# Expert tail and the next mixer's projections in one block, the value projection first, norm weights applied at the transposed copy

## The chip, the cores and the metric

One core of one Trainium2 chip runs the program. The metric is device time in microseconds of one execution, as the median of several runs; lower is better.

## What is computed

Three layers run one after another on 512 tokens of 1024 channels, all in float32: a hybrid mixer (state space and attention), a differential-attention mixer, and an RWKV-7 time mix. Each layer is a mixer, a norm, a mixture of experts with two experts per token, and a second norm.

```python
x = layer_norm(ALPHA * x + mixer(x), ln1_g, ln1_b)
f = hier_moe(x, ...)                 # out = sum over 2 experts of weight * (act @ w_down)
x = layer_norm(ALPHA * x + f, ln2_g, ln2_b)
# layer_norm: (x - mean) * rsqrt(var + 1e-5) * g + b
# differential attention: q, k, v = split(x @ w_qkv, 3)
# time mix: xx = shift(x) - x;  xm[n] = x + xx * mu[n]
#   r, k, v = xm[0..2] @ w_rkv[0..2];  w, a, g from xm[3], xm[4], xm[5] through narrow matrices w1, a1, g1
```

## The kernel before

Tokens lie in four tiles of 128 (`NT` = 4); `x_tok` holds them with tokens on the partitions and `xT` (in `xt_mem`) holds the transposed copy, eight blocks of 128 channels (`NK` = 8) by 512 tokens. Weights come in chunks of 2 MB (1024 rows by 512 columns) through `ring`, which has six slots; SP issues their loads in the order of a list, `stream`, and waits before each for the job that used the slot last (`used`). `first` is the list's first chunk of a mixer.

The program is a row of blocks. All engines meet at the end of a block before any starts the next. Around the change they are these.

- `project_and_experts` (L877) ends with a block of expert loops. In it the two rows of each token are written to the buffer `xybuf` in device memory; ACT's last stores must have landed before the block ends.
- The **tail** is the second block of the same function (L1300 to L1358). POOL gathers the expert rows of each tile by two indirect DMAs, eight in all (L1320), and behind the first pair it loads the norm weights as rows broadcast to all partitions, two loads of 512 KB (L282, L283). ACT scales `x_tok` by alpha (L1330). For each tile DVE adds the two weighted rows (L1347, L1348) and measures mean and variance (L222, L224); ACT takes the square root (L247); DVE normalizes (L229, L230) and multiplies by g (L231); POOL adds b (L252), for the last tile DVE (L234). DVE does a tile's measuring before it normalizes the tile before. PE turns each finished tile (L267, eight transposes of 128x128), ACT copies the result from PSUM in two activations (L273). SP loads three more chunks of the next mixer when all gathers have landed (L163); the first three came during the expert loops.
- `qkv_stage` (L1369) is the next block for the second layer: 24 jobs of PE, each eight k-steps into one PSUM bank (L1403), 16 for q and k, then 8 for v; ACT evacuates (L1414) and begins with an exponential for lambda (L1409).
- `rkv_stage` (L1464) is the next block for the third layer. ACT issues eleven parameter loads (L1546), PE turns the small parameters (L1513), DVE computes the token shift `xx` (L1498, L1499) and then six mixes of eight operations each (L1506), in the order w, a, g, r, k, v. PE runs four narrow jobs w, a, g, g2 (L1527), 16 jobs for r and k (L1539) and 8 for v (L1536), ACT evacuates (L1573).
- In the last layer nothing follows the tail, and SP stores each finished tile (L1313).

The first norm of each layer, in the expert stage, already works in another way: DVE makes scale and shift of a tile (L1169, L1170), ACT applies them in one activation (L1117), PE turns the tile (L1008), and DVE multiplies by g and adds b later (L1175, L1176). PE's projection jobs there are L1035.

## Time and profile before

| | us |
|---|---|
| median of 3 runs | 2915.38 (2912.75 to 2915.76) |
| the profiled execution, its own time | 2915.37 |
| its span in the trace | 2913.6 |

The span is the profiled stretch on the core; a row with a start time counts from its beginning. PE is TensorE's matmuls, PEld its weight loads, DVE is VectorE, ACT ScalarE, POOL GpSimd and SP SyncE. An arrow names what ended an engine's idle time.
### The profile page before, as it was taken

How to read it: one execution, taken by the hardware profiler on the slowest of the kernel's cores; microseconds unless marked ns; L12 is line 12 of the kernel's file. 1: busy time of each engine (PE TensorE's matmuls, PEld its weight loads, DVE VectorE, ACT ScalarE, POOL GpSimd, SP SyncE). 2: the span in 40 equal slices, each digit the busy share in tenths (PEclk: the TensorE clock that was granted, in tenths of full speed). 3: DMA queues.
4: the chain of work that ended last, by engine and by line, in shares of the span. 5: the costliest groups of instructions: out<-in, count | busy, mean ns of one | idle time of the engine just before them, and what ended most of it. 6: DMA issues, size and time to landing. Idle time of an engine off the chain costs nothing. (4 is left out here: it accounts for less than half of the span.)

```text
span 2913.6 us, 88815 instructions
## 1 busy us (share of the span) xinstructions
PE 2390.6 (82%) x39032; PEld 1652.3 (57%) x39033; DVE 1080.5 (37%) x2763; ACT 480.8 (17%) x1070; POOL 167.0 (6%) x254
## 2 busy tenths in 40 slices
PE   8987897999679978799866719988887889788972
PEld 3436656777534554577645513438787357566751
DVE  0205534333330284433311254016665743222325
ACT  1023411101110241110000010013333110000001
POOL 0000010000110000000000030001111200000002
PEclk9988899999889999999988959989999699899986
DMA  6211217987332101979999950000000349999994
GB/s 232 87 58 49 85 49 295 385 350 315 135 118 87 58 1 33 384 315 393 428 429 428 428 199 29 29 0 3 3 3 14 145 156 402 429 428 428 413 429 168
DMA packets 84523, 613.58 MB, mean 211 GB/s; under 512 B 20178, under 2 KB 41938, under 8 KB 50596
## 3 DMA queue, kind: packets, MB, share of 16 engines
q1 hardware_dynamic: 41440, 567.30, 47.0%
q10 hardware_dynamic: 36356, 22.86, 2.6%
q0 software_dynamic: 6592, 21.45, 2.3%
q8 instruction: 106, 1.74, 0.2%
q14 instruction: 29, 0.24, 0.0%
HBM read 579.04 MB, written 32.51 MB: 210 GB/s over the span
## 5 line engine op out<-in xcount | busy, mean ns | idle before, releaser
L1084 PE MATMUL ps<-ring,arena 128*32 128x128 f32 x13440 | 414.1, 282 | 110.7 <-DMA ring<-in_experts 80.9
L1084 PEld LDWEIGHTS ps<-ring,arena 128*32 128x32 f32 x13440 | 384.9, 114 | 152.0 <-DMA ring<-in_experts 78.9
L1061 PE MATMUL ps<-x_tok,arena 128*32 128x256 f32 x4832 | 305.2, 392 | 20.9 <-DVE arena L1198 16.7
L1284 DVE TENSOR_TENSOR arena<-arena,ps 128x64 f32<-128x64 f32 x296 | 65.6, 222 | 631.5 <-ACT arena L1143 631.5
L1143 ACT ACTIVATE arena<-ps 128x64 f32<-128x64 f32 x296 | 66.1, 223 | 1159.7 <-PE ps L1084 1159.7
L1061 PEld LDWEIGHTS ps<-x_tok,arena 128*32 128x32 f32 x4832 | 165.9, 114 | 103.8 <-issue 34.7
L1084 PE MATMUL ps<-arena 128*32 128x128 f32 x5504 | 178.8, 291 | 47.0 <-DMA arena<-in_experts 39.0
L1094 PE MATMUL ps<-ring,arena 128*32 128x256 f32 x3360 | 203.3, 380 | 8.4 <-DMA ring<-in_experts 8.1
L1084 PEld LDWEIGHTS ps<-arena 128*32 128x32 f32 x5504 | 163.4, 117 | 67.4 <-DMA arena<-in_experts 46.3
L1035 PE MATMUL ps<-ring,arena 128*128 128x512 f32 x384 | 168.4, 594 | 3.1 <-PEq L192 3.1
L1094 PEld LDWEIGHTS ps<-ring,arena 128*32 128x32 f32 x3360 | 112.9, 110 | 81.0 <-DMA ring<-in_experts 16.0
L1271 DVE STREAM_TRANSPOSE arena<-ps 128x256 f32<-128x256 f32 x151 | 67.9, 450 | 162.2 <-PE ps L1061 162.2
L1035 PEld LDWEIGHTS ps<-ring,arena 128*128 128x128 f32 x384 | 71.5, 190 | 87.2 <-issue 86.9
L1403 PE MATMUL ps<-xt_mem,ring 128*128 128x512 f32 x256 | 111.9, 600 | 0.9 <-PEq L1302 0.9
L1539 PE MATMUL ps<-arena,ring 128*128 128x512 f32 x256 | 110.1, 592 | 0.0
L453 PE MATMUL ps<-xt_mem,ring 128*128 128x512 f32 x256 | 110.0, 592 | 0.0
L846 DVE TENSOR_REDUCE small<-ps 128x1 f32<-128x128 f32 (+3 forms) x96 | 46.7, 486 | 167.5 <-PE ps L757 165.6
L1320 POOL DMA_INDIRECT arena<-xybuf,arena x24 | 24.1, 1004 | 1363.8 <-POOLq L951 861.0
L1295 DVE COPY arena<-ps 128x256 f32<-128x256 f32 x148 | 62.8, 425 | 88.0 <-PE ps L1094 88.0
L1094 PE MATMUL ps<-xt_mem,arena 128*32 128x256 f32 x1376 | 83.4, 380 | 6.5 <-DMA xt_mem<-in_experts 4.8
L1403 PEld LDWEIGHTS ps<-xt_mem,ring 128*128 128x128 f32 x256 | 49.3, 193 | 63.2 <-issue 63.2
L1539 PEld LDWEIGHTS ps<-arena,ring 128*128 128x128 f32 x256 | 48.6, 190 | 61.6 <-issue 61.6
(405 smaller groups left out, 3098.4 us busy)
## 6 DMA issues: line engine op xcount, KB each, us to landing
ring<-in_experts SPq DMA_DIRECT2D x165, 2048.0 KB, 22.1
arena<-in_experts SPq DMA_DIRECT2D x50, 2048.0 KB, 25.9
xt_mem<-in_experts SPq DMA_DIRECT2D x25, 2048.0 KB, 30.2
ring<-in_mixer_chunks SPq DMA_DIRECT2D x24, 2048.0 KB, 12.5
xybuf<-arena ACTq DMA_DIRECT2D x640, 32.0 KB, 6.7
xybuf<-arena SPq DMA_DIRECT2D x1, 9216.0 KB, 25.7
rows<-in_ln_g POOLq DMA_DIRECT2D x6, 512.0 KB, 5.2
rows<-in_ln_b POOLq DMA_DIRECT2D x6, 512.0 KB, 6.5
```

Of the source, the lines that this page charges most:

```text
L453: ins = pe.matmul(bank, w[:, k, j * P:(j + 1) * P], xT[:, k, :], start=(k == 0), stop=(k == NK - 1))
L846: link(dve.tensor_reduce(m[:, c:c + 1], score(n, c), AX, ALU.max))
L1035: ins = pe.matmul(ps[:, 2 * j + c, :], mT[:, k, j * P:(j + 1) * P], w[:, k, :], start=(k == 0), stop=(k == NK - 1))
L1061: ins = pe.matmul(ps[to, 5, 0:W], one_hot[:, j, :], x_tok[:, j, q * W:(q + 1) * W], start=(j == 0), stop=(j == NT - 1))
L1084: ins = pe.matmul(ps[at, 2 + half, 0:P], xg[:, k, :], w_gu[half][:, k, q, :], start=(k == 0), stop=(k == NK - 1))
L1094: ins = pe.matmul(ps[at, 4, 0:W], hT[:, f, :], w_d[:, f, q * W:(q + 1) * W], start=(f == 0), stop=(f == NT - 1))
L1143: act.activation(silu_g[:, half, :], ps[:, 2 + half, 0:HALF], ACT.Silu).then_inc(s_silu[half], 1)
L1271: dve.transpose(xg.rearrange("p k s -> p (k s)"), ps[:, 5, 0:W]).then_inc(s_xg, 1)
L1284: dve.tensor_tensor(hidden[:, half, :], silu_g[:, half, :], ps[:, 2 + half, HALF:P], ALU.mult)\
L1295: dve.tensor_copy(y_sb[:, b, :], ps[:, 4, 0:W]).then_inc(s_y, 1)
L1403: ins = pe.matmul(ps[:, n % 8, :], lhs, rhs, start=(k == 0), stop=(k == NK - 1))
L1539: ins = pe.matmul(bank, w[:, k, j * P:(j + 1) * P], xm[:, k, :], start=(k == 0), stop=(k == NK - 1))
```

## The change

For layers two and three the tail and the projection stage become one block (`norm_qkv_stage`, `norm_rkv_stage`); the last layer gets `last_norm_stage`. The chunks of the second and third mixer are listed with the value weights first. For each tile PE turns x as normalized but without g and b; ACT copies the turned tile in eight activations that apply g and b as columns (`take_rows`), and `x_tok` gets g and b from DVE afterwards (`gain_rows`). PE puts the turning of tile n+1 behind value job n. The norm rows and columns are loaded by POOL in the expert block. Gathered rows lie in ring slots. The third layer's parameters are loaded by SP into a ring slot at the block's start, and the value mix is made tile by tile. The exponential for lambda is moved to the end of its stage. "..." marks what is left out.

```diff
-            stream += [a["mixer_chunks"][8 * n + c] for c in range(8)]
+            stream += [a["mixer_chunks"][8 * n + c] for c in ((0, 1, 2, 3, 4, 5, 6, 7) if n == 0 else (4, 5, 0, 1, 2, 3, 6, 7))]
...
+        def gather_rows(pool, y1, y2, slots_i):
+            for j in range(NT):
+                for n, y in enumerate((y1, y2)):
+                    pool.indirect_dma_start(out=y[:, j, :], out_offset=None, in_=xybuf,
+                                            in_offset=bass.IndirectOffsetOnAxis(ap=slots_i[:, n, j:j + 1], axis=0))\
+                        .then_inc(rows_in[j].sem, 16)
+        def alpha_rows(act, alpha):
+            for j in range(NT):
+                act.activation(x_tok[:, j, :], x_tok[:, j, :], ACT.Copy, scale=alpha).then_inc(act_a.sem, 1)
+        def update_rows(dve, link, j, n0, y1, y2, w1, w2):
+            xj, mv = x_tok[:, j, :], mean_var[:, j, :]
+            dve.wait_ge(act_a.sem, n0["alpha"] + j + 1)
+            dve.wait_ge(rows_in[j].sem, n0["rows"][j] + 32)
+            link(dve.scalar_tensor_tensor(xj, y1[:, j, :], w1[:, j:j + 1], xj, ALU.mult, ALU.add))
+            link(dve.scalar_tensor_tensor(xj, y2[:, j, :], w2[:, j:j + 1], xj, ALU.mult, ALU.add))
             for c in range(2):
                 ins = dve.bn_stats(sums[:, j % 2, 6 * c:6 * c + 6], x_tok[:, j, c * CH:(c + 1) * CH])
             link(ins)
+            dve.bn_aggr(mv[:, 0:2], sums[:, j % 2, :]).then_inc(stat.sem, 1)
             dve.wait_ge(sq.sem, n0["sq"] + j + 1)
             link(dve.reciprocal(mv[:, 3:4], mv[:, 2:3]))
+            dve.tensor_scalar(mv[:, 1:2], mv[:, 0:1], mv[:, 3:4], -1.0, ALU.mult, ALU.mult).then_inc(scaled.sem, 1)
-            link(dve.tensor_scalar(xj, xj, mv[:, 0:1], mv[:, 3:4], ALU.subtract, ALU.mult))
-            ins = dve.tensor_tensor(xj, xj, g_row, ALU.mult)
-            if j == NT - 1:
-                link(ins)
-                ins = dve.tensor_tensor(xj, xj, b_row, ALU.add)
-            ins.then_inc(scaled.sem, 1)
...
+        def norm_rows(act, j, n0):
+            mv = mean_var[:, j, :]
             act.wait_ge(stat.sem, n0["stat"] + j + 1)
+            act.activation(mv[:, 2:3], mv[:, 1:2], ACT.Sqrt, bias=eps_ln).then_inc(sq.sem, 1)
+            act.wait_ge(scaled.sem, n0["scales"] + j + 1)
+            act.activation(x_tok[:, j, :], x_tok[:, j, :], ACT.Identity, bias=mv[:, 1:2], scale=mv[:, 3:4]).then_inc(ln_done.sem, 1)
+        def turn_rows(pe, j, n0):
+            pe.wait_ge(ln_done.sem, n0["normed"] + j + 1)
             for c in range(2):
                 for k in range(4):
                     at = (4 * c + k) * P
                     ins = pe.transpose(ps[:, 2 * j + c, k * P:(k + 1) * P], x_tok[:, j, at:at + P], ident)
                 ins.then_inc(tr.sem, 1)
+        def take_rows(act, j, n0):
             for c in range(2):
+                act.wait_ge(tr.sem, n0["turned"] + 2 * j + c + 1)
+                for k in range(4 * c, 4 * c + 4):
+                    ins = act.activation(xT[:, k, j * P:(j + 1) * P], ps[:, 2 * j + c, (k % 4) * P:(k % 4 + 1) * P], ACT.Identity,
+                                         scale=g_col[:, k:k + 1], bias=b_col[:, k:k + 1])
+                ins.then_inc(act_b.sem, 1)
+        def gain_rows(dve, link, j):
+            xj = x_tok[:, j, :]
+            link(dve.tensor_tensor(xj, xj, g_row, ALU.mult))
+            return dve.tensor_tensor(xj, xj, b_row, ALU.add)
...
+                    pool.wait_ge(*at_step("placed", LAST_TILE_SCALED))
+                    load_norm_rows(pool, g_src_2, b_src_2)
+                    if not last:
+                        load_norm_cols(pool, g_src_2, b_src_2)
...
+        def after_experts(n):
+            first = mixer_at[n]
+            return first, view(slot((first + 4) % SLOTS), 0, NT, D), view(slot((first + 5) % SLOTS), 0, NT, D)
+        def last_norm_stage(alpha, w1, w2, slots_i):
+            y1, y2 = view(arena, NK * T, NT, D), view(arena, 2 * NK * T, NT, D)
...
+                    def finish(j):
+                        dve.wait_ge(ln_done.sem, n0["normed"] + j + 1)
+                        gain_rows(dve, link, j).then_inc(dve_b.sem, 1)
+                    dve.wait_ge(loaded.sem, l0)
+                    for j in range(NT):
+                        update_rows(dve, link, j, n0, y1, y2, w1, w2)
+                        if j > 0:
+                            finish(j - 1)
+                    finish(NT - 1)
...
+        def norm_qkv_stage(alpha, w1, w2, slots_i):
+            first, y1, y2 = after_experts(1)
+            jobs = [(c, j) for j in range(NT) for c in range(2)] + [(c, j) for c in range(2, 6) for j in range(4)]
...
+                    load_chunk(sp, first + 3)
+                    sp.wait_ge(stat.sem, n0["stat"] + NT)
+                    for n in range(first + 4, first + SLOTS):
+                        load_chunk(sp, n)
...
+                    turn_rows(pe, 0, n0)
+                    for n, (c, j) in enumerate(jobs):
+                        if c < 2:
+                            pe.wait_ge(act_b.sem, n0["taken"] + 2 * j + 2)
+                        else:
...
+                        if n < NT - 1:
+                            turn_rows(pe, n + 1, n0)
...
+                    alpha_rows(act, alpha)
+                    act.wait_ge(loaded.sem, l0)
+                    for j in range(NT):
+                        norm_rows(act, j, n0)
+                        take_rows(act, j, n0)
+                    for n, (c, j) in enumerate(jobs):
+                        act.wait_ge(mm.sem, m0 + n + 1)
+                        dst = v2[:, j, c * CH:(c + 1) * CH] if c < 2 else (q2, k2)[(c - 2) // 2][:, 4 * (c % 2) + j, :]
+                        act.activation(dst, ps[:, n % 8, :], ACT.Copy).then_inc(ev.sem, 1)
                     act.wait_ge(dve_a.sem, x0 + 1)
+                    act.activation(sums_of, sums_of, ACT.Exp).then_inc(act_a.sem, 1)
...
+            buf = {"v": k3, "w": rT, "a": k3, "g": rT, "r": k3, "k": xx}
+            lora = slot((first + 3) % SLOTS)
+            jobs = [("v", c, j) for j in range(NT) for c in range(2)] + ["w", "a", "g", "g2"]
+            jobs += [(n, c, j) for n in "rk" for c in range(2) for j in range(4)]
...
+                    sp.wait_ge(consts.sem, c0 + 1)
+                    load(param_rows[0:6 * NK, :], a["rw_mu_2"][0].rearrange("n (k p) -> (n k) p", p=P))
...
+                    load(lora_w, a["rw_w1_2"][0].rearrange("(k p) n -> p k n", p=P))
+                    load(lora_a, a["rw_a1_2"][0].rearrange("(k p) n -> p k n", p=P))
+                    load(lora_g, a["rw_g1_2"][0].rearrange("(k p) n -> p k n", p=P))
+                    sp.wait_ge(stat.sem, n0["stat"] + NT)
+                    for n in range(first + 4, first + SLOTS):
+                        load_chunk(sp, n)
+                    sp.wait_ge(dve_b.sem, d0 + 1)
+                    load(w2a2[0:64, :], a["rw_w2_2"][0])
+                    load(w2a2[64:128, :], a["rw_a2_2"][0])
+                    sp.wait_ge(mm.sem, m0 + done["g2"])
+                    load_chunk(sp, first + 3)
...
+                    def mix_tile(j):
+                        of = slice(j * P, (j + 1) * P)
+                        if j == 0:
+                            dve.wait_ge(consts.sem, c0 + 3)
+                        dve.wait_ge(act_b.sem, n0["taken"] + 2 * j + 2)
+                        if j == 0:
+                            dve.tensor_tensor(xx[:, :, 1:P], xT[:, :, 0:P - 1], xT[:, :, 1:P], ALU.subtract)
+                            link(dve.tensor_scalar(xx[:, :, 0:1], xT[:, :, 0:1], -1.0, None, ALU.mult))
+                        else:
+                            link(dve.tensor_tensor(xx[:, :, of], xT[:, :, j * P - 1:(j + 1) * P - 1], xT[:, :, of], ALU.subtract))
+                        mix(0, of)
+                    for j in range(NT):
+                        update_rows(dve, link, j, n0, y1, y2, w1, w2)
+                        if j > 0:
+                            mix_tile(j - 1)
+                    mix_tile(NT - 1)
+                    mix(1, slice(0, T))
+                    dve.wait_ge(loaded.sem, l0)
+                    for j in range(NT):
+                        ins = gain_rows(dve, link, j)
+                    ins.then_inc(dve_b.sem, 1)
+                    for n, free_after in ((2, "v"), (3, "w"), (4, "a")):
+                        dve.wait_ge(mm.sem, m0 + done[free_after])
+                        mix(n, slice(0, T))
+                    mix(5, slice(0, T))
...
+                    pe.wait_ge(mixer_params.sem, p0 + 16 * 9)
                     pe.transpose(ps[:, 7, 0:P], param_rows, ident).then_inc(tr.sem, 1)
...
+                        if n < NT - 1:
+                            if n == NT - 2:
+                                pe.wait_ge(consts.sem, c0 + 3)
+                            turn_rows(pe, n + 1, n0)
...
+                    alpha_rows(act, alpha)
                     act.wait_ge(tr.sem, t0 + 1)
                     act.activation(mu, ps[:, 7, 0:6 * NK].rearrange("p (n k) -> p n k", n=6), ACT.Copy)
                     act.activation(par, ps[:, 7, 6 * NK:(6 + N_PAR) * NK].rearrange("p (n k) -> p n k", n=N_PAR), ACT.Copy)\
                        .then_inc(consts.sem, 1)
+                    act.wait_ge(loaded.sem, l0)
+                    for j in range(NT):
+                        norm_rows(act, j, n0)
+                        take_rows(act, j, n0)
```

## Rows read from the trace of the kernel before
**Rows 1.** The page: busy time, share of the span and instructions of each engine
```profile
PE 2390.6 (82%) x39032; PEld 1652.3 (57%) x39033; DVE 1080.5 (37%) x2763; ACT 480.8 (17%) x1070; POOL 167.0 (6%) x254
```
**Rows 2.** Timeline 774 to 800 us: start, length, engine, line, operation, [idle before <- releaser]
```profile
781.63 1.04 POOL L1320 DMA_INDIRECT arena<-xybuf,arena  x1 [345.62 <-POOLq L951]
...
788.29 1.28 DVE L1347 SCALAR_TENSOR_TENSOR x_tok<-arena,x_tok 128x1024 f32<-128x1024 f32 x1 [11.07 <-DMA arena<-xybuf,arena]
...
792.68 1.29 DVE L222 BATCH_NORM_STATS2 small<-x_tok 128x6 f32<-128x512 f32 x2 [1.79 <-DMA rows<-in_ln_b]
```
**Rows 3.** Timeline 800 to 835 us, the rest of the first tail
```profile
802.87 3.24 DVE L1348 SCALAR_TENSOR_TENSOR x_tok<-arena,x_tok 128x1024 f32<-128x1024 f32 x1
...
805.09 1.97 PE L267 MATMUL ps<-cst,x_tok 128*128 128x128 f32 x8 [28.35 <-POOL x_tok L252]
...
826.39 1.28 ACT L1409 ACT_TABLE_LOAD   x1 [0.26 <-PEq L1302]
...
826.42 8.93 PE L1403 MATMUL ps<-xt_mem,ring 128*128 128x512 f32 x16 [0.93 <-PEq L1302]
```
**Rows 4.** Timeline 1690 to 1800 us, second tail and the projections after it
```profile
1692.26 1.28 DVE L1347 SCALAR_TENSOR_TENSOR x_tok<-arena,x_tok 128x1024 f32<-128x1024 f32 x1 [11.30 <-DMA arena<-xybuf,arena]
...
1730.18 4.42 DVE L1498 TENSOR_TENSOR arena<-xt_mem 128x4088 f32<-128x4088 f32 x1 [2.95 <-PEq L1302]
...
1734.68 0.34 ACTq L1546 DMA_DIRECT2D rows<-in_rw_mu  x1
...
1746.24 0.48 PE L1513 MATMUL ps<-cst,rows 128*128 128x128 f32 x1 [16.98 <-DMA rows<-in_rw_a]
...
1752.60 15.22 PE L1527 MATMUL ps<-arena 128*64 128x512 f32 x32 [5.89 <-DVE arena L1506]
...
1762.65 10.69 DVE L1506 SCALAR_TENSOR_TENSOR arena<-arena,xt_mem 128x512 f32<-128x512 f32 x16 [4.80 <-PE ps L1527]
```
**Rows 5.** Timeline, the last evacuation of either projection stage
```profile
993.33 0.60 ACT L1414 ACTIVATE arena<-ps 128x512 f32<-128x512 f32 x1 [6.27 <-PE ps L1403]
...
1947.25 0.60 ACT L1573 ACTIVATE arena<-ps 128x512 f32<-128x512 f32 x1 [6.27 <-PE ps L1536]
```
**Rows 6.** Timeline 1125 to 1130 us, the first tile's norm in the expert stage
```profile
1125.73 0.16 DVE L1169 RECIPROCAL small<-small 128x1 f32<-128x1 f32 x1 [0.36 <-ACT small L1111]
1125.93 0.21 DVE L1170 TENSOR_SCALAR small<-small 128x1 f32<-128x1 f32 x1
...
1126.88 1.04 PE L1008 MATMUL ps<-cst,x_tok 128*128 128x128 f32 x8
...
1128.48 1.24 ACT L1117 ACTIVATE x_tok<-x_tok,small 128x1024 f32<-128x1024 f32 x1
```
**Rows 7.** Timeline 2855 to 2914 us, the last tail, DVE alone
```profile
2874.92 1.28 DVE L1347 SCALAR_TENSOR_TENSOR x_tok<-arena,x_tok 128x1024 f32<-128x1024 f32 x1 [11.91 <-DMA arena<-xybuf,arena]
...
2882.40 1.28 DVE L1347 SCALAR_TENSOR_TENSOR x_tok<-arena,x_tok 128x1024 f32<-128x1024 f32 x1 [1.40 <-DMA arena<-xybuf,arena]
...
2886.36 0.21 DVE L224 BATCH_NORM_AGGREGATE small<-small 128x2 f32<-128x12 f32 x1
...
2909.32 1.23 DVE L234 TENSOR_TENSOR x_tok<-x_tok,rows 128x1024 f32<-128x1024 f32 x1
```
**Rows 8.** Groups by shape, ACT and DVE, 128 columns: count, busy us, mean ns, idle before
```profile
L818 ACT ACTIVATE xt_mem<-ps,small 128x128 f32<-128x128 f32 x24 | 8.8, 367 | 6.9 <-DVE small L847 5.9 <-PE ps L776 0.7
...
L828 ACT ACTIVATE xt_mem<-ps 128x128 f32<-128x128 f32 x16 | 4.3, 267 | 0.0
...
L858 DVE SCALAR_TENSOR_TENSOR xt_mem<-xt_mem,small 128x128 f32<-128x128 f32 x8 | 2.8, 352 | 0.3
```
**Rows 9.** Windows: length, PE, PEld, DVE, ACT, POOL busy, TensorE clock, DMA share, GB/s
```profile
792.00:794.00 2.00, 0.00 (x0) 0.00 (x0) 1.29 (x2) 0.00 (x0) 0.94 (x1) 0.50 1.02 408
1190.00:1194.00 4.00, 3.35 (x96) 2.54 (x92) 1.28 (x5) 0.22 (x1) 0.00 (x0) 0.76 0.66 243
2398.00:2402.00 4.00, 4.00 (x120) 3.19 (x116) 1.64 (x5) 0.10 (x1) 0.00 (x0) 1.00 0.04 10
```

More of the change, by code:

```diff
@@ L216, in build, with tail_bases @@
         sums = view(lnx, 16, 2, 12)
-        def measure(dve, link, j):
+        def tail_bases():
+            return {"alpha": act_a.take(NT), "stat": stat.take(NT), "sq": sq.take(NT), "scales": scaled.take(NT), "normed": ln_done.take(NT),
+                    "turned": tr.take(2 * NT), "taken": act_b.take(2 * NT), "rows": [r.take(32) for r in rows_in]}
+        def gather_rows(pool, y1, y2, slots_i):
[13 more added lines that the diff above has]
+            link(dve.scalar_tensor_tensor(xj, y2[:, j, :], w2[:, j:j + 1], xj, ALU.mult, ALU.add))
             for c in range(2):
@@ L283, in load_norm_rows, with load_norm_cols @@
             pool.dma_start(b_row, b_src.partition_broadcast(P)).then_inc(loaded.sem, 16)
+        def load_norm_cols(pool, g_src, b_src):
+            with nc.allow_non_contiguous_dma("one value per partition"):
+                pool.dma_start(g_col, g_src.rearrange("(k p) -> p k", p=P)).then_inc(loaded.sem, 16)
+                pool.dma_start(b_col, b_src.rearrange("(k p) -> p k", p=P)).then_inc(loaded.sem, 16)
+        g_col, b_col = small[:, 8:16], small[:, 16:24]
         R_PAD = 96
@@ L1297, in project_and_experts @@
                 x.take(16 * (E // 3))
-            r0, l1, x0, n0 = loaded.take(32), [r.take(32) for r in rows_in], act_a.take(NT), norm_bases(not last)
-            o0 = stored.take(16 * NT) if last else 0
+            loaded.take(32 if last else 64)
+            return w1, w2, slots_i
+        def after_experts(n):
[3 more added lines that the diff above has]
+            y1, y2 = view(arena, NK * T, NT, D), view(arena, 2 * NK * T, NT, D)
+            n0, l0, d0, o0 = tail_bases(), loaded.total, dve_b.take(NT), stored.take(16 * NT)
             with nc.Block() as block:
@@ L1367, in build @@
         subln = rows[:, 256:256 + P]
[L1369 to L1371 removed]
+        def norm_qkv_stage(alpha, w1, w2, slots_i):
+            first, y1, y2 = after_experts(1)
+            jobs = [(c, j) for j in range(NT) for c in range(2)] + [(c, j) for c in range(2, 6) for j in range(4)]
+            n0, l0, lam0, d0 = tail_bases(), loaded.total, loaded.take(32), dve_b.take(1)
+            m0, e0 = mm.take(24), ev.take(24)
             for c in range(6):
[L1373 removed]
+                used[first + c] = (mm.sem, m0 + max(n for n, job in enumerate(jobs) if job[0] == c) + 1)
             prods = view(rows, 512, 2, HD)
[L1375 removed]
+            sums_of = cols[:, 16:18]
             x0, a0 = dve_a.take(1), act_a.take(1)
```

220 lines of the change are left out of this document (69 added, 151 removed).

## The prediction

> **What bounds the kernel now.** The page comes first: PE is busy 82% of the span [rows 1], so time is won only where PE stands still, and the change touches the three tails, where it does. In the timeline of the first tail POOL issues the first gather at 781.63, DVE begins the first tile at 788.29, and then waits 1.79 us more for the b row [rows 2]. PE's first transpose comes at 805.09 after 28.35 us of idleness, and its first projection at 826.42 [rows 3]. Between lies a chain: four tiles measured, normalized, shifted by POOL and turned, and nothing of the projection until the last has landed. One link is slow for a reason outside itself: L1348 takes 3.24 us while POOL adds b, against 1.28 for the same kind of operation in L1347 [rows 2, 3]. The second tail is the same with more behind it: DVE starts at 1692.26, the shift is computed from 1730.18, the first parameter load is issued at 1734.68, PE turns the parameters at 1746.24, having waited 16.98 us for a load, and its first job starts at 1752.60 [rows 4]. Both projection stages are then bound by PE: ACT evacuates a bank every 6.27 + 0.60 = 6.87 us, to the last at 993.33 and 1947.25 [rows 5]. So in either stage the question is when the first job starts, what is put between jobs, and what stands behind the last. The last tail has no projection; DVE's own chain ends it.
>
> **Layer two, start of the first job.** A tile's update by DVE runs from 2882.40 to the end of the aggregate at 2886.57 [rows 7], 4.17 us; behind it come ACT's root (0.36 idle), the reciprocal 0.16 and the scale 0.21 [rows 6], with a 0.04 handoff 0.77: **4.94 us an update**. Then ACT normalizes, 1.24 [rows 6], 0.1 for the handoff. PE turns the tile in 1.97 us at the 1.2 GHz that it has after idling (the same eight took 1.04 at 2.4 GHz) [rows 3, 6]. Then eight small copies stand where two wide ones stood. The trace has no copy with both scale and bias columns; the nearest are 0.267 us with none and 0.367 with a column [rows 8]. I take 0.35 apart; four of them overlap the second half of the turning but end about 0.5 after it, four more need 1.4, so about 2.0 behind PE.
> The start of the update moves too. SP now issues a 2 MB chunk at the block's start, where before it waited for the gathers. At the 408 GB/s that the DMA engines reach when full [rows 9] it takes 5.1 us. If the gather's packets come first it costs nothing, if the chunk goes first 5.1; a gain is excluded, since nothing that stood before the first pair is removed. I take 2.5, the middle, since both are in flight at once. So 788.3 + 2.5 + 4.94 + 1.34 + 2.0 + 2.0 = **801.1** for the first job against 826.4: 25.3 us won. It starts cold as before (8.93 for the first sixteen instructions [rows 3]), so that loss is in both.
> Between jobs PE turns tiles 1 to 3: 3 x 1.04 = 3.1 us back. They do not wait: tile 1 is normalized at about 804, during the first job; tile 2's root waits on ACT for the copies of tile 1, some 2 us after that turn, and is done inside the second job of 6.87. The v weights are there, for the first three chunks came in the expert loops. Behind the last job the exponential for lambda comes with its table load, 1.28 [rows 3], and four short steps of the size of those in [rows 6], 0.8 together: 2.1 back. DVE's g and b (8 operations of 1.23 [rows 7]) and the lambda loads queued behind them on POOL lie beside 165 us of matmuls. Layer two: 25.3 - 3.1 - 2.1 = **20.1 us**.
>
> **Layer three.** The parameters are loaded while rows are gathered, by SP, 1.2 MB up to the narrow matrices. Before, the whole set needed 11.6 us from first issue to PE's transpose [rows 4]. Issued from about 1685.6 (as far ahead of DVE's first update as in the first tail, 6.7 us [rows 2]), they land at 1697 at that pace, and ACT needs them before its first root, at 1698.4 (their copy is queued ahead of it). If all 4 MB of gathers went first, 10.3 us at 408 GB/s, they would come at 1707 and hold all back by 8.8. Bounds 0 and 8.8; I take 2, since most of the set is small and both queues move together. First tile copied: 1692.3 + 2 + 4.94 + 1.34 + 2.0 + 2.0 = 1704.6. DVE's second update is measured by then, but its root stands behind those copies: 1705.4. Only then comes the value mix of tile 0: a quarter of the shift (4.42 / 4 = 1.1 [rows 4]), 0.3 for the first column, and eight operations of at most 0.352 [rows 8], 0.3 apart with overlap: 3.8. First job at **1709.2** against 1752.6: 43.4 won.
> From there DVE needs about 8 to 9 us a tile (4.17 to measure, a wait for ACT, 3.5 to 3.8 to mix), and PE has two jobs and a transpose a tile, 14.8, so mixes stay ahead. Mix w (half of 10.69 us for 16 [rows 4]) and g and b are done before the eight v jobs end. Mix a can start only when v is done, as it reuses that buffer, and takes 5.3 beside job w of 6.87; g and r likewise. Their cover is thin, 1.5 us. Chunk first+3 is loaded only after g2, with four r jobs, 27.5 us, to hide it. The three turns cost 3.1 again: 43.4 - 3.1 = **40.3 us**.
>
> **Last tail.** The norm rows no longer stand between gathers, 1 MB at 408 GB/s, 2.5 us: the second tile's update starts at 2879.9 instead of 2882.40, just when the first is done (2874.92 + 4.94). Then three updates, 14.8, and four times g and b at 2.46, 9.8 (ACT normalizes beside them), end at 2904.6. Before it was 2909.32 + 1.23 = 2910.55 [rows 7]: **5.9 us**. POOL's adding was free there but slowed L1348; doing it on DVE costs less than it returns.
>
> **Expert blocks.** Each takes up 1 MB of norm rows, and small columns, when the routing is done. In the third layer the DMA engines carry 10 GB/s in 2398 to 2402, so there is room. In the second a third of the capacity was free in 1190 to 1194 (share 0.66), about 1.4 us of the 2.5 [rows 9]. Bounds 0 and 3 x 2.5 = 7.5; I take 0.5, as loads run well ahead of use at that point.
>
> **The sum.** 20.1 + 40.3 + 5.9 - 0.5 = 65.8. The profiled execution took 2915.37, as much as the median, and 1.8 us of it lie outside its span: 2915.4 - 65.8 = **2849.6**.
>
> **A rule beside the rows.** In the second tail the narrow matrices w1 and a1 arrive in rows of 64 floats, 256 bytes, 0.5 MB together. The Trainium skill, DMA: Bandwidth & Descriptors, Specifications, gives 512 bytes as the least for full rate. By that rule these two cost about twice their bytes, some 1.3 us more of DMA time, and the sum would be 2850.9; no row here isolates them.
>
> **Rivals.** A, transfers starve the first tile. For: the timeline puts the chunk and the parameters in the same microseconds as the gathers. Against: POOL's issue of a pair, not bandwidth, begins the chain. With 5.1 in layer two and 8.8 in layer three the time is 2849.6 + 2.6 + 6.8 = 2859.
> B, handoffs between PE, ACT and DVE set the pace in the value jobs. If each small copy costs 0.6 and PE waits at every tile, that is 2 us at either start and 1 us at each of six turns: 2859.6. Against: the slack computed above.
> C, the overlap is better than taken: no contention, copies 0.3 apart: 2849.6 - 2.5 - 2 - 0.5 - 1 = 2843.6.
> D, slower than before: TensorE's clock. After idling it is at 1.2 GHz (window 792 to 794 shows 0.50 [rows 9]), and it rose within the first job of unbroken work [rows 3]. Now transposes and waits stand between the value jobs. If it never rises in them, each costs 6.87 more: 16 jobs, 110 us, less the 4 us already in, 2849.6 + 106 = 2956. It decides from ten such jobs on, where 68.7 us eats the gain. Against: expert stages alternate the same turns and jobs at 1.04 us a turn, full clock [rows 6].
> The Trainium skill, TensorE: Matmul & The Clock Gate, HAM oscillation, describes this failure where every group of matmuls ends in a wait; by it the time would be rival D's.
>
> **Chances.** Forecast 0.69, A 0.12, B 0.08, C 0.08, D 0.03. The range reaches from C, less 3 us for sums of handoffs, to both upper DMA bounds with the experts' 7.5: 2840 to 2866; it leaves out D and the worst of A and B together. No change is what a measurement can't tell from 0.2%, 6 us. Faster 0.96, same 0.01, slower 0.03.
>
> **What would show it.** In the new profile: the first projection matmul some 20 us after the first gather's issue in layer two and 24 in layer three; its predecessor's idle time down by 25 and 43; no waits of PE for DVE or ACT above 1 us between value jobs; clock 1.00 from the second job; L1348's kind at 1.28 everywhere; a table load behind layer two's last evacuation; DVE's last operation 30 us after its first in the last tail. The prediction is wrong if the first gather lands more than 5 us later than before, if DVE's mixing of a tile outlasts two jobs, or if expert loops grow by more than 3 us a layer.

## The result, and the profile after

The changed kernel takes **2862.31 us** (median of 4 runs, 2861.22 to 2863.58) against 2914.95 (4 runs): ratio 0.982, 95% interval 0.9804 to 0.9836. It is 52.6 us faster; the forecast was 65.8, the range reached to 2866. The profiled execution took 2863.58 with a span of 2861.7, so 51.9 us of span were won, 13.9 less than forecast.

The page, busy time of each engine, answers to [rows 1]. PE does the same work in a shorter span; POOL no longer adds b in the tails, ACT got the small copies.

```profile
PE 2390.6 (84%) x39032; PEld 1654.0 (58%) x39033; DVE 1070.0 (37%) x2799; ACT 509.6 (18%) x1130; POOL 139.5 (5%) x248
```

The timeline of the changed kernel, layer two's tail up to the second job and the stage's end, answers to [rows 2, 3, 5].

```profile
780.16 0.20 ACT L1154 ACTIVATE small<-cst 128x1 f32<-128x1 f32 x1 [6.86 <-DMA xybuf<-arena]
780.61 0.33 SPq L163 DMA_DIRECT2D ring<-in_mixer_chunks  x1
781.37 1.05 POOL L227 DMA_INDIRECT ring<-xybuf,arena  x1 [331.07 <-POOLq L955]
...
791.54 1.28 DVE L240 SCALAR_TENSOR_TENSOR x_tok<-ring,arena,x_tok 128x1024 f32<-128x1024 f32 x1 [14.59 <-DMA ring<-xybuf,arena]
...
795.50 0.21 DVE L245 BATCH_NORM_AGGREGATE small<-small 128x2 f32<-128x12 f32 x1
795.79 1.28 ACT L254 ACT_TABLE_LOAD   x1 [11.26 <-DVE small L245]
797.09 0.30 ACT L254 ACTIVATE small<-small,cst 128x1 f32<-128x1 f32 x1
...
799.15 1.97 PE L264 MATMUL ps<-cst,x_tok 128*128 128x128 f32 x8 [22.68 <-ACT x_tok L256]
800.31 2.90 ACT L272 ACTIVATE xt_mem<-ps,small 128x128 f32<-128x128 f32 x8 [1.21 <-PE ps L264]
803.26 10.12 PE L1399 MATMUL ps<-ring,xt_mem 128*128 128x512 f32 x16 [2.14 <-ACT xt_mem L272]
813.23 1.04 PE L264 MATMUL ps<-cst,x_tok 128*128 128x128 f32 x8
814.10 7.03 PE L1399 MATMUL ps<-ring,xt_mem 128*128 128x512 f32 x16
...
973.99 0.60 ACT L1414 ACTIVATE arena<-ps 128x512 f32<-128x512 f32 x1 [6.27 <-PE ps L1399]
974.60 1.28 ACT L1416 ACT_TABLE_LOAD   x1
976.78 1.19 PE L760 MATMUL ps<-cst 128*128 128x128 f32 x4 [2.83 <-PEq L1367]
```

Tiles are turned between jobs in 1.04 us without a wait, as meant. Two things were not in the forecast: a table load stands between the variance (795.50) and the root (797.09), and behind the exponential the next block's first matmuls take 1.19 us for four, where the kernel before took 0.68.

The same view, layer three, answers to [rows 4]:

```profile
1673.57 0.20 ACT L1154 ACTIVATE small<-cst 128x1 f32<-128x1 f32 x1 [6.83 <-DMA xybuf<-arena]
...
1683.08 1.28 DVE L240 SCALAR_TENSOR_TENSOR x_tok<-ring,arena,x_tok 128x1024 f32<-128x1024 f32 x1 [12.68 <-DMA ring<-xybuf,arena]
...
1687.04 0.21 DVE L245 BATCH_NORM_AGGREGATE small<-small 128x2 f32<-128x12 f32 x1
1693.42 0.47 PE L1569 MATMUL ps<-cst,ring 128*128 128x128 f32 x1 [23.52 <-DMA ring<-in_rw_g]
...
1695.55 0.29 ACT L254 ACTIVATE small<-small,cst 128x1 f32<-128x1 f32 x1
...
1705.79 9.42 PE L1594 MATMUL ps<-ring,arena 128*128 128x512 f32 x16 [6.20 <-DVE arena L1535]
```

The variance of tile 0 is there at 1687.2, and its root starts 8.3 us later: ACT waits for the turned parameters before it, and PE, which turns them, waits for the ninth load of the parameters (`in_rw_g`).

To compare runs, the span is cut at marks that every kernel has: the end of an expert block (ACT's small ACTIVATE above), the first attention matmul, the first 128x512 matmul of the attention's projection, and POOL's memset that opens the wkv block. All lengths are differences of start times in the profiled execution, in us. `e1` to `e8` and the last two are the experiments below.

| kernel | to first mark | layer two tail + projection | attention | experts | layer three tail + projection | wkv + experts | last tail |
|---|---|---|---|---|---|---|---|
| before | 780.4 | 213.8 | 112.0 | 577.9 | 264.0 | 918.1 | 47.4 |
| after | 780.2 | 196.6 | 115.2 | 581.6 | 230.0 | 918.1 | 40.1 |
| e1 exponential early | 778.1 | 194.6 | 112.4 | 580.5 | 229.3 | 916.2 | 39.9 |
| e2 chunk late | 777.9 | 193.1 | 115.2 | 581.5 | 229.9 | 916.6 | 40.4 |
| e3 parameters split | 781.4 | 196.6 | 115.2 | 581.5 | 223.1 | 918.2 | 40.1 |
| e4 rows late | 779.1 | 196.2 | 115.1 | 579.1 | 232.6 | 916.3 | 40.0 |
| e5 root's table | 782.1 | 193.6 | 113.9 | 581.1 | 230.3 | 918.3 | 39.8 |
| e6 turns first | 778.0 | 208.4 | 113.7 | 581.2 | 229.9 | 916.6 | 39.9 |
| e7 warm end | 781.7 | 196.1 | 111.9 | 580.7 | 229.8 | 916.8 | 39.9 |
| e8 warm start | 778.3 | 193.0 | 115.1 | 581.9 | 229.6 | 914.3 | 39.9 |
| five moves | 777.7 | 188.5 | 112.2 | 579.1 | 221.7 | 919.4 | 40.0 |
| five moves, warm | 781.5 | 186.5 | 111.0 | 578.4 | 218.9 | 915.1 | 40.0 |

Each row is one execution. The first and the sixth length move by 4 to 5 us between executions whatever the edit, the others by up to 1.4 (experts), 1.2 (attention, in the two rows of five moves) or 1 where the edit doesn't touch them. So a price of 2 us is read from a stage, not from a whole time, and a price under 1.4 us only from the rows of a timeline. Against before, layer two gave 17.2, layer three 34.0 and the last tail 7.3, while attention took 3.25 and the experts 3.6 back.

### The profile page after: what moved, and what is told of

Same layout as the page of the kernel before. It is cut to its first block and busy times, and to the rows that moved or that the text cites. A ratio compares the mean times of both kernels' runs of the same rounds, so it can differ in the third digit from the quotient of the medians.

```text
span 2861.7 us, 88888 instructions
## 1 busy us (share of the span) xinstructions
PE 2390.6 (84%) x39032; PEld 1654.0 (58%) x39033; DVE 1070.0 (37%) x2799; ACT 509.6 (18%) x1130; POOL 139.5 (5%) x248
## 5 line engine op out<-in xcount | busy, mean ns | idle before, releaser
L1090 PE MATMUL ps<-ring,arena 128*32 128x128 f32 x13440 | 420.2, 285 | 111.9 <-DMA ring<-in_experts 79.0
L459 PEld LDWEIGHTS ps<-xt_mem,ring 128*128 128x128 f32 x256 | 48.6, 190 | 61.2 <-issue 61.2
L1399 PEld LDWEIGHTS ps<-xt_mem,ring 128*128 128x128 f32 x256 | 48.6, 190 | 61.2 <-issue 61.2
L1293 DVE STREAM_TRANSPOSE arena<-arena 128x64 f32<-128x64 f32 x296 | 72.8, 246 | 10.1
```

The lines of the kernel that those rows point to most:

```text
L459: ins = pe.matmul(bank, w[:, k, j * P:(j + 1) * P], xT[:, k, :], start=(k == 0), stop=(k == NK - 1))
L1090: ins = pe.matmul(ps[at, 2 + half, 0:P], xg[:, k, :], w_gu[half][:, k, q, :], start=(k == 0), stop=(k == NK - 1))
L1293: dve.transpose(hT[:, 2 * half:2 * half + 2, :].rearrange("p f s -> p (f s)"), hidden[:, half, :])\
L1399: ins = pe.matmul(ps[:, n % 8, :], lhs, rhs, start=(k == 0), stop=(k == NK - 1))
```

## Experiments

Line numbers are those of each kernel. Every kernel is the changed one with the edit shown.

**e1: the exponential before the last eight evacuations.**

```diff
                     for n, (c, j) in enumerate(jobs):
+                        if n == 12:
+                            act.wait_ge(dve_a.sem, x0 + 1)
+                            act.activation(sums_of, sums_of, ACT.Exp).then_inc(act_a.sem, 1)
                         act.wait_ge(mm.sem, m0 + n + 1)
...
-                    act.wait_ge(dve_a.sem, x0 + 1)
-                    act.activation(sums_of, sums_of, ACT.Exp).then_inc(act_a.sem, 1)
```

> The changed kernel with the exponential for lambda moved from behind the last evacuation of layer two's projections to between the evacuations of jobs 12 and 13. Theory: the step behind the last job costs twice, 2.05 us of length (0.94 to 2.83 us of PE idle) and then a clock that falls to 1.2 GHz at the start of the attention block (granted 0.59 and 0.50 in its first 6 us), some 3.2 us more. Expected: PE idle before the first attention matmul back at 0.9 to 1.0 us, its first four transposes 0.68 us instead of 1.19, the stretch from the end of the expert block to the first attention matmul shorter by 2 us and the attention block by 3; 2857 us. Rival: the attention block's 3 us come from something else (order of loads, DMA traffic in its first microseconds), then only 2 us go and the clock stays low: 2860 us.

Measured: 2855.91 us (2852.88 to 2860.09), ratio 0.9804 (0.9787 to 0.982). The stage falls by 2.0 us and the attention behind it by 2.9. The timeline of e1, PE at the start of attention:

```profile
972.67 0.68 PE L760 MATMUL ps<-cst 128*128 128x128 f32 x4 [0.94 <-PEq L1367]
```

PE idles 0.94 us instead of 2.83, and its first four matmuls are back at 0.68. The wait costs twice: once itself, once in what follows. e7 tests whether that second part is the clock.

**e7: PE kept busy through the same wait.** The exponential stays behind the last job.

```diff
                         if n < NT - 1:
                             turn_rows(pe, n + 1, n0)
+                    pe.wait_ge(ev.sem, e0 + 17)
+                    for k in range(3):
+                        pe.matmul(ps[:, 0, :], ident, xT[:, k, :], start=(k == 0), stop=(k == 2))
```

> Edit: kernel after, with three matmuls of 128x512 (six instructions of 0.43 us, 2.6 us together) issued by PE behind layer two's last projection job, into a bank that is free; their result is used by nobody. They fill PE's idle time while ACT computes the exponential for lambda. Theory: that idle time of 2.83 us costs twice, once by itself and once since the granted clock falls to 0.50 to 0.6 in the first microseconds of the attention block; with PE kept busy the tail and projection stay at 196.6, and the attention stage falls from 115.2 to 112.4 as in the run with the exponential moved. Rival: the attention stage is longer in after because of something else the exponential's place brings (the order of ACT's work or late data), and stays at 115.2. If the six instructions were to hold the attention block back, the first stage would grow by up to 0.5.

Measured: 2858.99 (2858.28 to 2862.21), ratio 0.9812 (0.9798 to 0.9825). The stage is 196.1, no longer than with PE idle, and attention is 111.9 instead of 115.2. Windows of 2 us from the first attention matmul (length, PE, PEld, DVE, ACT, POOL busy, TensorE's clock, DMA share, GB/s); first the changed kernel:

```profile
976.78:978.78 2.00, 2.00 (x9) 1.55 (x9) 0.04 (x1) 0.00 (x0) 0.00 (x0) 0.50 0.95 410
978.78:980.78 2.00, 2.00 (x12) 1.71 (x12) 0.75 (x4) 0.85 (x4) 0.00 (x0) 0.50 0.93 397
980.78:982.78 2.00, 2.00 (x14) 1.62 (x12) 1.60 (x7) 1.08 (x4) 0.00 (x0) 0.50 0.06 16
982.78:984.78 2.00, 2.00 (x17) 1.34 (x17) 1.24 (x4) 0.33 (x1) 0.00 (x0) 0.85 0.00 0
```

and e7, where transfers run just as hard beside it:

```profile
977.72:979.72 2.00, 2.00 (x17) 1.64 (x18) 0.80 (x4) 0.35 (x2) 0.00 (x0) 1.00 1.00 426
```

PE issues 9 matmuls in the first 2 us at 1.2 GHz and 17 at 2.4, with the exponential where it was and the transfers as before. So the second cost is the clock's: the theory is confirmed and the rival falls.

**e2: chunk first+3 of layer two behind the gathers.**

```diff
-                    load_chunk(sp, first + 3)
                     sp.wait_ge(stat.sem, n0["stat"] + NT)
-                    for n in range(first + 4, first + SLOTS):
+                    for n in range(first + 3, first + SLOTS):
```

> The changed kernel with layer two's load of chunk first+3 issued behind the wait for the variances, so that it does not meet the gathers. Theory: the first gather landed 3.5 us later than before the change because it shared the DMA engines with this 2 MB load. Expected: DVE's first update 3 to 3.5 us earlier (7.9 us after the end of the expert block instead of 11.4), first value job as much earlier, 2859 us. Rival: the gather is late for another reason (rows written to ring slots, eight gathers without the norm loads between them): the update starts where it did, 2862 us.

Measured: 2857.49 (2856.47 to 2858.21), ratio 0.9805 (0.9789 to 0.9821). In e2's timeline DVE's first update starts 7.88 us after the mark at 777.92:

```profile
785.80 1.28 DVE L240 SCALAR_TENSOR_TENSOR x_tok<-ring,arena,x_tok 128x1024 f32<-128x1024 f32 x1 [11.09 <-DMA ring<-xybuf,arena]
```

In the changed kernel it is 11.38, in the kernel before it was 7.87. The 2 MB chunk delays the first pair by 3.5 us, and the whole 3.5 arrives at the stage's end (196.6 to 193.1).

**e3: the third layer's parameters in two groups.** The six small loads get a semaphore of their own; the narrow matrices are waited for at job w.

```diff
-                    load(param_rows[0:6 * NK, :], a["rw_mu_2"][0].rearrange("n (k p) -> (n k) p", p=P))
+                    sp.dma_start(param_rows[0:6 * NK, :], ...).then_inc(mix_rows.sem, 16)
...
-                    pe.wait_ge(mixer_params.sem, p0 + 16 * 9)
+                    pe.wait_ge(mix_rows.sem, 16 * 6)
...
+                        if job == "w":
+                            pe.wait_ge(mixer_params.sem, p0 + 16 * 3)
```

> The changed kernel, with layer three's six small parameter loads on a semaphore of their own; PE turns them when they have landed and waits for the three narrow matrices only before job w. Theory: PE's turn of the parameters (19 us behind the first issue) and with it ACT's first root, 8.2 us late, wait for the narrow matrices, whose packets share the engines with 4 MB of gathers; the small ones land early. Expected: the parameters turned before the first variance, root of tile 0 within 2 us of the variance (with its table load), first value job 6 to 7.5 us earlier, 2855.5 us. Rival: the small loads are themselves held up behind the gathers (short rows, full queues): the root stays over 5 us late, gain below 3 us, 2860 us.

Measured: 2854.15 (2853.03 to 2857.9), ratio 0.9791 (0.9775 to 0.9808). The timeline of e3, with the mark at 1674.59:

```profile
1680.74 0.47 PE L1571 MATMUL ps<-cst,ring 128*128 128x128 f32 x1 [9.82 <-DMA ring<-in_rw_r_k]
...
1688.27 1.28 ACT L255 ACT_TABLE_LOAD   x1 [6.71 <-DVE small L246]
1689.56 0.29 ACT L255 ACTIVATE small<-small,cst 128x1 f32<-128x1 f32 x1
```

The parameters are turned 6.2 us after the mark instead of 19.9, before the first rows are there, so no tile waits for them any more, and the stage falls by 6.9. It was not the vectors that were late but three matrices that the same count included and that nobody needs before job w. With them out of the way the table load stands in the open here too.

**e4: norm rows behind the gathers**, not in the expert block, in both joint blocks.

```diff
-                    load_norm_rows(pool, g_src_2, b_src_2)
-                    if not last:
+                    if last:
+                        load_norm_rows(pool, g_src_2, b_src_2)
+                    else:
                         load_norm_cols(pool, g_src_2, b_src_2)
...
                     gather_rows(pool, y1, y2, slots_i)
+                    load_norm_rows(pool, a["ln2_g"][0], a["ln2_b"][0])
```

> The changed kernel with the 1 MB of norm rows of layers one and two loaded behind the gathers of the tail, not in the expert block (the columns stay there; the last layer is as in the changed kernel). Theory: in layer two's expert block this 1 MB costs 3 us, since weights stream at the DMA engines' full rate at that point and PE waits 2.65 us for a chunk about 20 us in. Expected: from first attention matmul to the end of that expert block 693.5 us instead of 696.8, the rows hidden in the tails (needed only when all tiles are updated), 2859.5 us. Rival: the 3 us come from the chunks' other order or phase, not the rows: 2862 us, or slower if the rows delay gathers.

Measured: 2861.17 (2860.32 to 2862.32), ratio 0.9818 (0.9802 to 0.9834): 1.1 us less than the changed kernel, which is not clear of noise, but two stages moved. Experts 581.6 to 579.1, layer three 230.0 to 232.6. Windows of 10 us, 80 to 110 us into the attention projection and expert block, columns as above. The kernel before:

```profile
1186.20:1196.20 10.00, 8.39 (x180) 5.91 (x184) 4.28 (x23) 1.73 (x3) 0.00 (x0) 0.71 0.81 292
1196.20:1206.20 10.00, 9.26 (x236) 7.36 (x228) 3.43 (x12) 0.45 (x2) 0.00 (x0) 1.00 0.99 416
1206.20:1216.20 10.00, 8.00 (x204) 5.68 (x199) 2.96 (x11) 0.45 (x2) 0.00 (x0) 1.00 1.00 419
```

The changed kernel:

```profile
1172.00:1182.00 10.00, 8.43 (x180) 5.97 (x184) 4.17 (x22) 1.73 (x3) 0.00 (x0) 0.70 1.06 384
1182.00:1192.00 10.00, 6.17 (x169) 4.60 (x165) 2.19 (x8) 0.22 (x1) 0.00 (x0) 0.98 1.01 417
1192.00:1202.00 10.00, 9.67 (x219) 8.29 (x222) 2.71 (x10) 0.68 (x3) 0.00 (x0) 0.85 1.01 427
```

And e4:

```profile
1170.37:1180.37 10.00, 8.05 (x176) 5.70 (x180) 4.36 (x24) 1.73 (x3) 0.00 (x0) 0.70 0.88 292
1180.37:1190.37 10.00, 8.32 (x217) 6.45 (x213) 2.83 (x10) 0.45 (x2) 0.00 (x0) 1.00 0.99 411
```

The 1 MB falls into a window with a fifth of the capacity free (0.81 before, 1.06 after), but the DMA engines are full from there on in either kernel (0.99 and 1.01), and PE's busy time in the next window drops from 9.26 to 6.17; in the one after it PE makes up a part (9.67 against 8.00). One execution could differ from another by 1.4 here, so the other rows of the table count too: the experts take 578.4 to 579.1 in the three kernels with the rows moved (e4 and both kernels of five moves) and 580.5 to 581.9 in the changed kernel and the seven others. Behind the gathers of layer three the same megabyte delays the narrow matrices: PE turns the parameters 22.7 us after the mark instead of 19.9. One stage pays what the other wins.

**e5: one wait before the first root.**

```diff
-                    act.wait_ge(loaded.sem, l0)
                     for j in range(NT):
                         norm_rows(act, j, n0)
+                        if j == 0:
+                            act.wait_ge(loaded.sem, l0)
                         take_rows(act, j, n0)
```

> Lengths are between markers, the end of an expert block, the first attention matmul and the memset of the next block. Kernel after: 196.6 for layer two's tail and projection, 230.0 for layer three's. Edit: in both joint blocks ACT's wait for the norm columns moves from before the first root to between the first normalizing and its copies, so that one wait stands before the root. Theory: the table load of 1.28 us stands behind the last wait of two and is not started before it; with one wait it is pulled ahead, as in the last tail. Then the root in layer two follows the first aggregate by some 0.1 us instead of 1.4, the first job comes 1.3 us earlier, layer two's stage is 195.3, and layer three's is unchanged, since the parameters' arrival sets it there. Whole kernel 1.3 us less than after, 2861. Rival: the load is placed right before the root whatever the waits, and both stages stay at 196.6 and 230.0.

Measured: 2857.62 (2854.52 to 2861.19), ratio 0.9804 (0.9791 to 0.9818). e5's timeline, ACT behind the mark at 782.05:

```profile
786.44 1.28 ACT L254 ACT_TABLE_LOAD   x1
797.26 0.29 ACT L254 ACTIVATE small<-small,cst 128x1 f32<-128x1 f32 x1 [9.54 <-DVE small L245]
```

The load runs ten microseconds early, and layer three does not change: theory confirmed, rival fallen. The stage fell by 3.0, more than the 1.3 expected: 1.3 from the root, 0.4 from a gather that came sooner, and 1.3 in the first job (8.78 against 10.12), whose cold part was shorter. Only the first is accounted for by the edit; nothing here shows that the other 1.7 are. The Trainium skill, ScalarE activation tables: per-element evaluation and per-set limits, What a function is on this engine, gives 1283 ns for a load. The rows here agree with 1.28; where the load stands among the waits is what the runs add.

**e6: all tiles of layer two turned before the first job.**

```diff
-                    turn_rows(pe, 0, n0)
+                    for j in range(NT):
+                        turn_rows(pe, j, n0)
...
-                        if n < NT - 1:
-                            turn_rows(pe, n + 1, n0)
```

> Edit: in layer two all four tiles are turned before the first projection job, as before the change; the shorter chain (no shift by b on POOL, norm weights at the copy) and the value-first order of jobs stay. Theory: most of the 23 us that the first job came earlier is overlap of the tiles' chains with jobs. A tile's period from normalizing to normalizing is 6.0 us in the kernel after, so the fourth tile is turned at 799.2 + 3 x 6.0 + 2.0 = 819.2 and the first job comes 15.9 us later than in after; the three turns of 1.04 no longer stand between jobs. Stage 196.6 + 15.9 - 3.1 = 209.4. Layer three unchanged. Rival: the gain is the shorter chain's (POOL's b out of the way of DVE and the narrower work), and turning tile by tile is worth little: the stage is under 202.

Measured: 2870.93 (2869.52 to 2872.88), ratio 0.9853 (0.9838 to 0.9868). PE's jobs in e6, with the mark at 778.02:

```profile
816.78 23.42 PE L1400 MATMUL ps<-ring,xt_mem 128*128 128x512 f32 x50
```

The first job starts 38.8 us after the mark (23.1 in the changed kernel, 46.0 before), and the stage is 208.4. So of 22.9 us by which the first job moved, 15.7 are the overlap of three tiles with jobs and 7.2 the shorter chain, net of the 3.5 by which the rows come late in both. In the length of the stage the overlap is worth 11.7 of the 17.2, since it puts three turns between jobs. The rival, that turning tile by tile is worth little, falls.

**e8: PE warmed before the first tile of layer two.**

```diff
+                    wait_chunk(pe, first)
+                    pe.wait_ge(rows_in[0].sem, n0["rows"][0] + 32)
+                    heat(pe, first, 6)
                     turn_rows(pe, 0, n0)
+                    heat(pe, first, 2)
```

(`heat` issues that many matmuls of 128x512 into bank 6, with results that nobody reads.)

> Edit: kernel after; in layer two PE, which idles 22.7 us before tile 0 is turned, issues six matmuls of 128x512 (twelve instructions) into a free bank once the first pair of rows is in, 7.6 us before that turn in after, and two more between the turn and the first job. Nobody uses their result. Theory: the cold clock costs 0.93 us at the turn (1.97 against 1.04) and up to 3.2 us at the first job (10.12 us against 6.87 + 0.04); kept at 2.4 GHz by this work the turn takes 1.04, the first job 6.9 to 7.1 and layer two's tail and projection 196.6 - 4.1 = 192.5. The copies that set the distance from turn to first job follow the turn, so its 0.93 shows in full. Rival one: the clock is still at 1.2 GHz after twelve instructions or falls again in the waits between; then nothing is won or the added work delays the turn by up to 2 us. Rival two: the 10.12 us of the first job are a wait for its weights and not the clock; then only 0.9 is won. Layer three and the attention stage as in after (230.0, 113.7 to 115.2).

Measured: 2854.17 (2853.59 to 2857.4), ratio 0.9796 (0.9783 to 0.9809). PE's timeline in e8:

```profile
789.60 7.16 PE L270 MATMUL ps<-ring,cst 128*128 128x512 f32 x12 [14.95 <-DMA ring<-xybuf,arena]
797.18 1.09 PE L264 MATMUL ps<-cst,x_tok 128*128 128x128 f32 x8 [0.43 <-ACT x_tok L256]
800.83 7.13 PE L1408 MATMUL ps<-ring,xt_mem 128*128 128x512 f32 x16 [0.83 <-ACT xt_mem L277]
```

The first job takes 7.13 instead of 10.12, the turn 1.09 instead of 1.97. Of the turn's 0.9 only 0.46 show (11.26 us from first update to first job, 11.72 in the changed kernel), since the copies start after its first half; expected was all of it. The stage fell by 3.6. Windows, columns as above; first the changed kernel, in its first job:

```profile
807.26:809.26 2.00, 2.00 (x3) 0.67 (x2) 0.62 (x2) 0.00 (x0) 0.00 (x0) 0.50 0.00 0
809.26:811.26 2.00, 2.00 (x6) 0.94 (x5) 0.00 (x0) 0.00 (x0) 0.00 (x0) 0.99 0.00 0
```

and e8, twice in the added work and once at the start of the first job:

```profile
791.60:793.60 2.00, 2.00 (x5) 0.73 (x4) 1.93 (x4) 0.00 (x0) 0.00 (x0) 0.61 1.04 416
793.60:795.60 2.00, 2.00 (x6) 0.94 (x5) 0.30 (x2) 1.58 (x2) 0.00 (x0) 1.00 1.00 399
800.83:802.83 2.00, 2.00 (x5) 1.04 (x6) 1.77 (x4) 1.36 (x2) 0.00 (x0) 1.00 0.00 0
```

Both rivals fall: the clock was the cause. It rose during the twelve instructions and was still at 1.00 when the first job began, which in the changed kernel it reached only some 6 us into that job.

**The five moves together (e1 to e5).**

> Edit: kernel after with five moves together: exponential before the last eight evacuations of layer two; chunk first+3 of layer two loaded behind the gathers; layer three's parameters in two groups with a semaphore each; norm rows of both joint blocks loaded behind their gathers instead of in the expert block; one wait before the first root. Theory: the prices found singly add up, since each is a link of another chain: layer two's stage 196.6 - 2.0 - 3.5 - 1.3 = 189.8 (less than that much if the second tile's link takes over), attention 112.4, experts 579.1, layer three 223.1 less up to 1.3 by the root's table, with the rows' delay of the narrow matrices now waited for only at job w, so 222 to 223. Sum 6.8 + 2.9 + 2.5 + 7.5 = 19.7 under after, about 2842. Rival: the delays overlap or take each other's place (rows behind the gathers again hold up what layer three needs, the root's table is hidden by the chunk's delay), and it is not under 2849.

Measured: **2840.51** (2837.91 to 2841.62), ratio 0.9743 (0.973 to 0.9757). Layer two 188.5, attention 112.2, experts 579.1, layer three 221.7: all four within 1.3 us of what was expected, so the prices add. The 1.3 is layer two's, where the first job took 8.52 instead of 10.12. In layer three the norm rows show no cost any more: the stage is 1.4 shorter than in e3, as the root's table alone would make it.

**The five moves with both joint blocks warmed.**

> Edit: the five moves together, and the same warming work in both joint blocks: five matmuls (ten instructions) before tile 0 is turned, two (layer two) or six (layer three, where DVE's shift and mixes take 6.3 us) between the turn and the first job. Theory: in the run of the five moves the turn took 1.97 and the first job 8.52 in layer two, 1.97 and 9.78 in layer three, so 0.9 + 1.6 and 0.9 + 2.9 are to be had: stages 188.5 - 2.5 = 186.0 and 221.7 - 3.8 = 217.9, the whole 2840.5 - 6.3 = 2834. Rival: the clock does not rise in ten instructions, or the 6.3 us between update and turn are too short for them, and the time is 2840 or more.

Measured: **2837.81** (2833.41 to 2841.34), ratio 0.9739 (0.9726 to 0.9752). Layer two falls by 2.0 and layer three by 2.8 against the five moves (2.5 and 3.8 were expected); the first jobs take 7.13 in either, where they took 8.52 and 9.78. The medians differ by 2.7, and the ratios' intervals overlap, so the whole times don't settle it; the jobs' lengths do. Against before it is 77.0 us or 2.6% faster, half as much again as the change.

## Why the prediction was right, and where 13.9 us went

The direction and the range held, and the chains were cut where the text said. The number of the likeliest case was 12.7 us too low; rival A's 2859 lay nearer, and its mechanism has the larger part in the gap. That the range held is in part luck: it was drawn for transfers and expert loops, while 5.7 us came from things that no term had (attention 3.25, ACT's table load 1.28, the longer cold first job 1.19). And one of the prediction's own signs of being wrong came true: expert loops that grow by more than 3 us a layer; the second layer's grew by 3.6. By the forecast's steps:

- **Layer two, first job** (forecast 20.7 us after the mark, by its 801.1; measured 23.1). The gather was taken as 2.5 late and is 3.5 (e2). ACT's table load, 1.28, was in no term: in the kernel before it ran while DVE waited for rows, and the forecast moved the root without asking what stands in front of it (e5). The small copies are 8 in 2.90, 0.36 apart, as taken.
- **The cold start**: "that loss is in both" was right in kind, but the first job took 10.12 where it had 8.93. Unwarmed, the first value jobs of the two joint blocks take 8.5 to 10.2 in these runs; what sets the length within that was not tested.
- **Turns**: from the start of a turn to the next job 0.87 (813.23 to 814.10) instead of 1.04; 0.5 better. Exponential tail 1.9 more instead of 2.1. Together 17.2 instead of 20.1.
- **Attention**: forecast at nothing, 3.25 lost. The step that failed is "2.1 back" for the exponential: the wait was priced at its own length only, though the same text had the clock at 0.50 after idle time in its cold start. e1 and e7 show it.
- **Expert blocks**: 0.5 taken, 3.6 measured in the second layer. For the first and the third nothing can be said: the lengths that hold them are the same within 0.2 (780.4 and 780.2, 918.1 in both), but these two move by 4 to 5 between executions. "Loads run well ahead of use at that point" was wrong: one window with room was read, not the full ones behind it. e4 gives 2.5 of it to the norm rows, as much as the megabyte takes at full rate. The other 1.2 stay open and are within what this length moves by; the norm columns, loaded in the same place, were not tried alone.
- **Layer three**: 34.0 instead of 40.3. Of the bounds 0 and 8.8 the forecast took 2, "since most of the set is small"; the root comes 8.3 us behind the variance. Most loads are small, but the wait counts nine, three of them matrices. A smaller part: DVE's first update comes 9.5 us after the mark where it came 8.1, and the forecast left it in its place. With the wait split (e3) the stage gains 40.9, near the forecast's number, but partly by luck: there the 2 us taken for the parameters are not spent at all, while the first update is still 1.3 late and the table load's 1.28 stand in the open. The cover called thin, for the mixes behind the value jobs, held: from the first value job at 1705.79 to the block's end PE waits for no other engine.
- **Last tail**: 7.3 instead of 5.9. Updates take 4.86 to the next, not 4.94, and the first pair lands 0.8 us sooner.

Rival A was mostly true: transfers held up the first tile by 3.5 of its 5.1 us in layer two (e2) and 6.9 of its 8.8 in layer three (e3). In layer three it is in part argued: e3 shows that the matrices were waited for, and e4's 2.8 us with 1 MB more in flight speaks for the transfers as what made them late, but how much their short rows did, the prediction's rule beside the rows, no run separates. It was given 0.12, since one row, the pair's issue, was taken to rule the start; it rules it only while the queues are otherwise empty. Rival B fell, with no wait between value jobs. Rival D fell as put: the clock was 1.00 from the second value job on, and the turns between them took 1.04 us. The Trainium skill, TensorE: Matmul & The Clock Gate, HAM oscillation, describes a clock that falls again where every group of matmuls ends in a wait; no value job ended in one, so these runs don't test that rule. A clock that falls after a wait did strike once, behind the last job, at 3.25 us against the rival's 106.

## What to carry to other kernels

Price a new wait on PE with what the clock does behind it, not with its length alone, and fill it with work that nobody needs if it can't be moved. When loads are moved to an earlier place, look at what the semaphore of a wait counts and whether the transfers are full in the microseconds behind the gap, and not only whether the gap has room. Prices of 2 to 7 us are measured in stages between marks; the whole time of this kernel moves by as much for other reasons.

## What was not expected of the hardware

- An idle time of 2.83 us on PE before attention came with a drop of TensorE to 1.2 GHz in seven profiles, 0.94 or 0.30 us with none in five. In five of the seven the block's first four matmuls took 1.19 to 1.20 us and attention 115.1 to 115.2; in e5 and e6 they still took 0.68, the mean clock of the first 2 us was 0.96 and 0.82 before it fell to 0.50, and attention took 113.9 and 113.7. So the same idle time cost a further 1.8 or 3.2 us behind it; what decides between the two was not tested.
- A 2 MB load issued 0.8 us ahead of the first gather delays that gather's rows by 3.5 us, though it takes 5.1 at the rate of [rows 9]. The chunk itself lands 8.9 us after its issue, and the median gather 8.7 after its own, against 6.0 in e2, where no chunk is in flight: both are slowed, so they share the engines and neither goes first.
- In these kernels the activation table load stands ahead of the root's wait where there is one and behind it where there are two: at 786.44 in e5, at 795.79, after the variance, in the changed kernel. Layer three agrees: with two waits it stands behind the variance in e3 (1688.27), with one ahead of DVE's first update in the kernel of five moves (1664.48 against 1666.62).
